# Two transformer layers as one block: borders crossed by token tile, gate and up products with the weights stationary

## What is computed

```
def hybrid_layer(x, c, ada_w, ada_b, ...):
    mod = jax.nn.silu(c) @ ada_w + ada_b
    sh_m, sc_m, g_m, sh_f, sc_f, g_f = [m[:, None, :] for m in jnp.split(mod, N_MOD, axis=-1)]
    h = rms_norm(x, norm_mix_g) * (1 + sc_m) + sh_m
    proj = h @ w_in
    ...
    merged = (jax.nn.sigmoid(ga) * (o_na @ w_br_na)
              + jax.nn.sigmoid(gb) * (o_mla @ w_br_mla)
              + jax.nn.sigmoid(gc) * (o_gqa @ w_br_gqa))
    x = x + g_m * (merged @ w_out)
    h = rms_norm(x, norm_ffn_g) * (1 + sc_f) + sh_f
    gate, up = jnp.split(h @ ffn_w_gate_up, 2, axis=-1)
    x = x + g_f * ((jax.nn.silu(gate) * up) @ ffn_w_down)
    return x
```

## Time and profile before

| | |
|---|---|
| median of 3 runs | 1840.91 us |
| the profiled execution's own time | 1846.1 us |
| its span, first to last instruction | 1844.3 us |
| TensorE matmuls busy | 88% of the span |
| VectorE busy | 66% |
| ScalarE busy | 44% |
| mean granted TensorE clock | 0.925 of full |

### The profile page before, as it was taken

One profiled execution on the slowest core, in us unless ns is written; L12 is line 12 of the kernel. 1 busy time (PEld: TensorE's weight loads), 2 busy tenths in 40 slices (PEclk: granted clock), 3 DMA queues, 4 the chain that ended last, 5 costly groups with the idle time before them and its releaser, 6 DMA issues. The chain is left out here.

```text
span 1844.3 us, 25528 instructions
## 1 busy us (share of the span) xinstructions
PE 1625.5 (88%) x10701; PEld 1469.1 (80%) x10701; DVE 1225.5 (66%) x1338; ACT 813.2 (44%) x921; POOL 35.7 (2%) x52
## 2 busy tenths in 40 slices
PE   2899998999899999899969997897698958999995
PEld 2789887999788988799969997885687856888884
DVE  4777577787656547566554876534565757898895
ACT  1345434333244543433323562225433316777673
POOL 0100000000010000000000000000000000000000
PEclk8899998999989999899989998987887968999998
DMA  8975337888744324466446462111222446999992
GB/s 307 298 231 159 139 118 258 296 305 301 248 140 146 114 89 154 169 206 227 139 122 200 143 183 92 46 46 46 85 76 69 137 139 217 367 358 359 355 358 108
DMA packets 226057, 348.07 MB, mean 189 GB/s; under 512 B 14612, under 2 KB 156672, under 8 KB 225808
## 3 DMA queue, kind: packets, MB, share of 16 engines
q1 hardware_dynamic: 225936, 346.36, 56.0%
HBM read 345.29 MB, written 1.97 MB: 188 GB/s over the span
## 5 line engine op out<-in xcount | busy, mean ns | idle before, releaser
L458 PE MATMUL bank<-layer_split,hT_pair 128*128 128x256 f32 (+1 forms) x4224 | 511.1, 281 | 9.9 <-DVE hT_pair L315 5.5
L458 PEld LDWEIGHTS bank<-layer_split,hT_pair 128*128 128x128 f32 x4224 | 496.9, 190 | 16.6 <-issue 9.3
L184 DVE TENSOR_TENSOR layer_split<-layer_raw,layer_split 128x2048 fp32r<-128x2048 f32 x122 | 280.2, 2296 | 99.0 <-ACT layer_split L172 97.4
L172 ACT ACTIVATE layer_split<-layer_raw 128x2048 fp32r<-128x2048 f32 x122 | 233.7, 1915 | 199.3 <-PE bank L458 114.4
L184 DVE TENSOR_TENSOR expert_split<-expert_raw,expert_split 128x2048 fp32r<-128x2048 f32 x96 | 219.4, 2289 | 40.8 <-ACT expert_split L172 40.7
L172 ACT ACTIVATE expert_split<-expert_raw 128x2048 fp32r<-128x2048 f32 x96 | 184.2, 1920 | 76.5 <-PE bank L1823 39.1
L458 PE MATMUL bank<-split_w,hT_pair 128*128 128x256 f32 (+1 forms) x1248 | 183.9, 311 | 13.9 <-PEq L2018 5.0
L458 PEld LDWEIGHTS bank<-split_w,hT_pair 128*128 128x128 f32 x1248 | 173.2, 207 | 25.1 <-issue 15.6
L184 DVE TENSOR_TENSOR split_w<-raw_w,split_w 128x2048 fp32r<-128x2048 f32 x52 | 119.2, 2292 | 66.8 <-ACT split_w L172 66.2
L672 PE MATMUL bank<-layer_split,ffnh_aT 128*128 128x512 f32 x528 | 127.0, 396 | 2.8 <-DVE ffnh_aT L744 2.8
L172 ACT ACTIVATE split_w<-raw_w 128x2048 fp32r<-128x2048 f32 x52 | 99.4, 1911 | 59.7 <-PE bank L458 52.4
(11 more groups left out here) (442 smaller groups left out, 1783.7 us busy)
## 6 DMA issues: line engine op xcount, KB each, us to landing
layer_raw<-in_ada_w SPq DMA_DIRECT2D x48, 1024.0 KB, 5.9
layer_raw<-in_ffn_w_gate_up SPq DMA_DIRECT2D x44, 1024.0 KB, 5.1
raw_w<-in_w_in SPq DMA_DIRECT2D x40, 1024.0 KB, 5.1
layer_raw<-in_w_in SPq DMA_DIRECT2D x38, 1024.0 KB, 6.1
expert_raw<-in_w_gate SPq DMA_DIRECT2D x32, 1024.0 KB, 7.2
expert_raw<-in_w_up SPq DMA_DIRECT2D x32, 1024.0 KB, 7.2
expert_raw<-in_w_down SPq DMA_DIRECT2D x32, 1024.0 KB, 6.9
layer_raw<-in_ffn_w_down SPq DMA_DIRECT2D x22, 1024.0 KB, 5.1
```

What stands on the lines that cost most here:

```text
L172: self.nc.scalar.activation(self.pair[:, j % self.pairs, 0, 0:self.size[n]], self.raw[:, n % self.depth, 0:self.size[n]], ACT.Copy).then_i ...
L184: self.nc.vector.tensor_tensor(self.pair[:, j % self.pairs, 1, 0:self.size[n]], self.raw[:, n % self.depth, 0:self.size[n]], self.pair[:, ...
L458: ins = nc.tensor.matmul(out, lhs, rhs, start=c == 0 and tp + wp == 0, stop=c == job.k - 1 and tp == 1)
```

## The change

Five things are done at once. (1) Both layers stand in one `nc.Block`; each engine runs `proj`, `att`, `ffn` of layer 0 and then of layer 1 with no barrier between. (2) At the borders the work goes by token tile: `SkewNorm` squares halves of a tile, normalises tile 0 and later tile 1, and ScalarE writes the scaled value, from which VectorE copies the high half and subtracts the low one. The output product is ordered by tile pairs; the transposes of the heads' results stand among the heads (three of four) and those of the merged sum among the branch products (`Merge`). (3) The gate and up products have the weights stationary and 256 tokens moving; their result has features on partitions, so the four transposes per block are gone. ScalarE applies SiLU in one activation (before, a sigmoid, and VectorE multiplied), VectorE multiplies once instead of twice, and the high half is copied from SBUF. (4) In the first block of each feed-forward part the tokens move by tile: `hidden_of_tile`, 192 products of 128 columns in place of 96 of 256. (5) The projections use their weight units in another order (2, 3, 0, 1, 4 ...).

```diff
-                for c0 in range(0, 1952, 256):
-                    w["proj"].append(add_cols("w_in", l, c0, min(c0 + 256, 1952)))
-                    ada_next(p)
+                w["proj"] = [None] * 8
+                for i in (2, 3, 0, 1, 4, 5, 6, 7):
+                    w["proj"][i] = add_cols("w_in", l, 256 * i, min(256 * i + 256, 1952))
+                    ada_next(p)
...
-                        attention(l, ring, w, cols_l[l], mods[l], Gm[l], gate_rows, ada, rows_loaded, make_strips, sg3, o_tok, x_in)
-                        merge(ring, w, sg3, o_tok, gate_rows[:, 0, :])
-                        norm = Norm("ffn", s2, ring, w["gu"][0][0], Gf[l], mods[l][:, 24:32])
-                        gated_hidden("ffnh", ring, (lambda n, up, w=w: w["gu"][n][up], lambda n, w=w: w["dn"][n]), n_hidden,
-                                     lambda n, t: None, norm=norm, ada=ada, sync_first=rows_ahead, gate=gate_rows[:, 1, :], tail=1 + l)
...
+                    def rows_ahead(sp, l=l, merge=merge):
+                        sp.wait_ge(merge.out_left.sem, 8)
+                        if l + 1 < DEPTH:
+                            load_gate_row(sp, l + 1, 2, rows_loaded)
+                            make_strips(sp, l + 1)
+                        load_gate_row(sp, l, 5, rows_loaded)
+                    ffn = FeedForward(ring, w, n_hidden, buf, ffn_norm[l], mix_norm[l + 1] if l + 1 < DEPTH else None, ada,
+                                      rows_ahead, gate_rows[:, 1, :])
+                    parts += [proj, att, ffn]
+                LAYER[0] = ""
...
+                    @block.tensor
+                    def _(pe):
+                        for part in parts:
+                            part.tensor(pe)
...
+            def flat(self, act, t, half):
+                act.wait_ge(self.turned, 2 * t + half + 1)
+                act.wait_ge(*self.scale_ready)
+                for k in range(4 * half, 4 * half + 4):
+                    ins = nc.scalar.activation(self.xn[t][:, k * P:(k + 1) * P], ps[4 + 2 * t + half][:, (k % 4) * P:(k % 4 + 1) * P],
+                                               ACT.Identity, bias=self.bias[:, k:k + 1], scale=self.scale[:, k:k + 1])
+                ins.then_inc(self.flat_out, 1)
+            def vector(self, dve, t, half):
+                dve.wait_ge(self.flat_out, 2 * t + half + 1)
+                src = self.xn[t][:, 512 * half:512 * half + 512].rearrange("p (k s) -> p k s", k=4)
+                hi, lo = (hP[:, i, 4 * half:4 * half + 4, t * P:(t + 1) * P] for i in range(2))
+                done(dve, nc.vector.tensor_copy(hi, src), self.split)
+                nc.vector.tensor_tensor(lo, src, hi.bitcast(FP), ALU.subtract).then_inc(self.lo_out, 1)
+            def ready(self, t):
+                def wait(pe, c):
+                    if c % 4 == 0:
+                        pe.wait_ge(self.lo_out, 2 * t + c // 4 + 1)
+                return wait
...
+                self.branch(pe, 10)
+                self.turn_half(pe, 2)
+                self.branch(pe, 11)
+                self.output(pe, 0)
+                self.turn_half(pe, 3)
+                for j in range(1, 7):
+                    self.output(pe, j)
+                self.output(pe, 7, lambda: self.norm.turn(pe, 0))
+                self.norm.turn(pe, 1)
...
+                self.hi_half(act, 3)
+                norm.square(act, 0, 0)
+                ring.hi(act, w["out"][3])
+                norm.square(act, 1, 0)
+                ring.hi(act, w["gu"][0][0])
+                norm.square(act, 0, 1)
+                norm.flat(act, 0, 0)
+                norm.flat(act, 0, 1)
+                norm.square(act, 1, 1)
+                ring.hi(act, w["gu"][0][1])
+                norm.flat(act, 1, 0)
+                norm.flat(act, 1, 1)
...
+                self.output_out(dve, 1)
+                ring.lo(dve, w["out"][3])
+                self.output_out(dve, 2)
+                self.output_out(dve, 3)
+                ring.lo(dve, w["gu"][0][0])
+                self.output_out(dve, 4)
+                self.output_out(dve, 5)
+                norm.norm(dve, 0)
+                self.output_out(dve, 6)
+                norm.vector(dve, 0, 0)
+                norm.vector(dve, 0, 1)
+                self.output_out(dve, 7)
+                ring.lo(dve, w["gu"][0][1])
+                norm.norm(dve, 1)
+                norm.vector(dve, 1, 0)
+                norm.vector(dve, 1, 1)
...
+                def hidden_of_tile(up, t):
+                    ring.arrived(pe, gu(0, up))
+                    weights = [ring.view(gu(0, up), wp, KD, UNIT_W) for wp in range(2)]
+                    for f in range(2):
+                        for c in range(KD):
+                            if up + f == 0:
+                                norm.ready(t)(pe, c)
+                            for tp, wp in ((0, 0), (0, 1), (1, 0)):
+                                ins = nc.tensor.matmul(ps[up][:, f * S + t * P:f * S + (t + 1) * P],
+                                                       weights[wp][:, c, f * P:(f + 1) * P], hP[:, tp, c, t * P:(t + 1) * P],
+                                                       start=c + tp + wp == 0, stop=c == KD - 1 and tp == 1)
+                    if t == 1:
+                        ins.then_inc(ring.used, 1)
...
+                for n in range(blocks):
+                    if n == 0:
+                        for up, t in ((0, 0), (1, 0), (0, 1), (1, 1)):
+                            hidden_of_tile(up, t)
+                    else:
+                        hidden(n, 0)
+                        hidden(n, 1)
+                    if n and ada.due(gu(n, 0)):
+                        ada.reduce(pe, 3, 1)
+                        self.reduced_in[n] = 1
+                    if n >= 1:
+                        down(n - 1)
+                down(blocks - 1)
+                while ada.due(ring.ahead(dn(blocks - 1), 1)):
+                    ada.reduce(pe, 3, 1)
+                self.ada_end = ada.done_pe
+                if self.norm_next is not None:
+                    self.norm_next.turn(pe, 0)
+                    self.norm_next.turn(pe, 1)
...
+                for n in range(self.blocks):
+                    ring.hi(act, ring.ahead(gu(n, 0), 2))
+                    act.wait_ge(ring.used, ring.uses(gu(n, 0)))
+                    if n >= 1:
+                        act.wait_ge(self.acted, n)
+                    nc.scalar.activation(self.sig.rearrange(flat), ps[0][:, :], ACT.Silu).then_inc(self.gated, 1)
+                    ring.hi(act, ring.ahead(gu(n, 0), 3))
+                    act.wait_ge(self.acted, n + 1)
+                    if n >= 1:
+                        act.wait_ge(ring.used, ring.uses(dn(n - 1)))
+                    ring.hi(act, ring.ahead(gu(n, 1), 3))
+                    nc.scalar.activation(self.aT[:, 0, :, :].rearrange(flat), self.a.rearrange(flat), ACT.Copy) \
+                        .then_inc(self.hi_out, 1)
+                    if n >= 1:
+                        ring.hi(act, ring.ahead(dn(n - 1), 3))
...
+                for n in range(self.blocks):
+                    ring.lo(dve, ring.ahead(gu(n, 0), 2))
+                    if n and self.reduced_in[n - 1]:
+                        ada.leave(dve, 3)
+                    ring.lo(dve, ring.ahead(gu(n, 0), 3))
+                    dve.wait_ge(self.gated, n + 1)
+                    dve.wait_ge(ring.used, ring.uses(gu(n, 1)))
+                    if n >= 1:
+                        dve.wait_ge(self.lo_out, n)
+                    nc.vector.tensor_tensor(self.a.rearrange(flat), ps[1][:, :], self.sig.rearrange(flat), ALU.mult) \
+                        .then_inc(self.acted, 1)
+                    ring.lo(dve, ring.ahead(gu(n, 1), 3))
+                    dve.wait_ge(self.hi_out, n + 1)
+                    nc.vector.tensor_tensor(self.aT[:, 1, :, :].rearrange(flat), self.a.rearrange(flat),
+                                            self.aT[:, 0, :, :].rearrange(flat).bitcast(FP), ALU.subtract).then_inc(self.lo_out, 1)
+                    if n >= 1:
+                        ring.lo(dve, ring.ahead(dn(n - 1), 3))
+                dve.wait_ge(self.tile_sum, 1)
+                self.add(dve, 0, 0)
+                self.add(dve, 0, 1)
+                dve.wait_ge(ring.used, ring.uses(dn(self.blocks - 1)))
+                self.add(dve, 1, 0)
+                if norm is not None:
+                    norm.norm(dve, 0)
+                self.add(dve, 1, 1)
+                while ada.done_dve < self.ada_end:
+                    ada.leave(dve, 3)
+                if norm is not None:
+                    norm.vector(dve, 0, 0)
+                    norm.vector(dve, 0, 1)
+                    norm.norm(dve, 1)
+                    norm.vector(dve, 1, 0)
+                    norm.vector(dve, 1, 1)
```

1202 lines of the change are left out of this document (774 added, 428 removed).

## The result

The changed kernel takes 1897.2 us (median of 4 executions, 1889.03 to 1900.38) against 1841.99 for the kernel before in the same series: ratio 1.0285, 95% interval 1.0259 to 1.0311. It is slower by 3%; I had forecast 1837.0 with a range to 1850. The profiled execution took 1895.74 us, its span is 1893.9, its mean granted clock 0.912.

The account below looks back on a forecast made before the run. Inside the stages TensorE was taken as the bound (transfers at the start). Terms 1.7 + 2.6 + 1.6 - 6.4 + 3.0 - 0.6 - 5.75 = -3.85 us gave 1842.2 on the profiled scale, 1837.0 on the median's; range 1826 to 1850.

Parts of the forecast that it names:

- The part between heads and output product: Layer 0, last head's transposes to the end of the output products: 55.0 us instead of 60.4, a gain of 5.4.
- The entry: Start of the feed-forward part: 8.5 us stop, then low clock and narrow products, 33.9 us against 26.75, loss 7.1.
- I take 5.5 in all, nearer to the unbroken case: Low-clock time after the feed-forward entry's stop: 2.0 us of transposes plus 3.5 us of products, bounded by 4.0 and 14.6.
- Rival B: Feed-forward entries: low clock outlasts 5.5 us, each further microsecond costing half; at 14.6 us, 9 us more, 1846; chance 0.20.
- Rival C: First feed-forward blocks: stationary loads hide, narrow products run at 0.09 us, 8.6 us less, 1828.4; chance 0.08.
- E: Feed-forward entries: ScalarE and VectorE run ahead, half of the two 8.5 us stops goes, 1828.5; chance 0.12.
- D: Steady blocks: 1.3 us slack fails, units come 2.5 us late, ten blocks lose 1.2 us each, 1849; chance 0.15.
- the term of -6.4: Steady feed-forward blocks: four transposes less save 0.36 us a block, nine blocks in each of two layers, -6.4 us.
- Weights or tokens stationary makes no difference: Steady feed-forward blocks: 256-column products were to take the same time with either operand stationary.
- Around the last down product: Stop ahead of it: 5.0 us in layer 0, +3.0; 1.4 us in layer 1, -0.6; layer 0's product takes 8.0 us.
- The border to layer 1: Last down product to the first 96 projection products: 9.3 us until tile 1 is turned, 32.1 against 37.85, -5.75 us.

Follow-up runs that it names:

- wide: Changed kernel with the first feed-forward block as 96 products of 256 columns, started once both tiles are split: 1843.3 us, ratio 1.0018 to the kernel before.
- narrow-first: Kernel before with only each layer's first feed-forward block made of 192 products of 128 columns instead of 96 of 256: 1892.5 us, ratio 1.0285.
- gate-wide: Changed kernel with the first block's gate product as 48 products of 256 columns, its up product still 96 of 128 behind it: 1849.4 us, one execution.
- the sixth block: Kernel before with only each layer's sixth feed-forward block made of 192 products of 128 columns instead of 96 of 256: 1862.0 us, ratio 1.0126.
- the tokens-stationary run: Changed kernel with tokens stationary and weights moving in gate and up products from the second block on, output not the reference's: 1882.5 us.
- the fastest version: Changed kernel with the feed-forward entry stop taken away, first up product 256 columns wide, ScalarE's high half ahead of its wait: 1833.5 us, ratio 0.9963.
- the run without the stop: Changed kernel, first block still narrow, with ScalarE and VectorE reordered and tile 1 turned after tile 0's first 48 products: 1844.9 us, ratio 1.0014.

## Why the prediction was wrong

**The part between heads and output product: wrong.** Forecast 55.0 us, measured 60.2 (222.59 to 282.80), so the gain of 5.4 never was. The waits were right (4.7 us idle for 4.3 and hops). The work was mis-sized, TensorE was busy 55.5 and not about 50 us. Twelve products of 512 columns behind the 0.95 us stop took 4.44 us, at the low clock (at my 0.229 each it would be 2.7), the rest 0.237 each; the output products come every 0.120 us and not 0.1145; the transposes of tile 0 ran at the low clock. For the 512-column products I had doubled a price of 256-column ones, though the kernel before has their own row, 0.238 each:

```profile
234.48 22.83 PE L458 MATMUL bank<-layer_split,merge_pair 128*128 128x512 f32 x96 [0.22 <-DVE merge_pair L315]
```

**The entry: the failed step.** The stop was right (8.01 and 7.82 us for 8.5), and so was the price of a narrow product at full clock. Wrong was "I take 5.5 in all, nearer to the unbroken case", with its reason that the low clock ends with unbroken work. Between the transposes' start and the rise of the clock lie 45.7 us of unbroken work. The wide, narrow-first and gate-wide runs show what was missing: the time at the low clock depends on what runs, and these products of 128 columns seldom end it. Both rows from which I bounded it, 4.0 and 14.6 us (14.9 by its own row, 0.57 being the mean of that microsecond), end in 256-column products; I carried the bound over to narrow ones without saying so. The cost is 42.6 us where I had 25.4, in each layer. The Trainium skill, TensorE: Matmul & The Clock Gate, What's actually happening, has the warm-up as a matter of time and not of how many products, with one count for 128 columns and one for 512. By that rule the clock would have been full early in the first block, and my 5.5 us were drawn up the same way. The trace disagrees (41.0 us at 0.50 with 128 columns, 3 to 5 us with 256), and the trace decides.

What it is about these products stays open, for 128 columns alone don't do it: in the kernel before, rows of 16 transposes of 128 columns see the clock rise within them, at 263.5 and 744.7. Widths between 128 and 256 weren't run. But the trace of the kernel before holds a warning that I passed over, in its second part: 16 transposes and 32 products of 16 columns, 10.3 us without a gap, and the clock stays at 0.50.

```profile
1500.50 3.68 PE L1682 MATMUL bank<-cst,x 128*128 128x128 f32 x16 [12.91 <-DVE x L1613]
1503.97 6.85 PE L1692 MATMUL bank<-router_w,hT 128*128 128x16 f32 x32
```

```profile
1500.50:1510.80 10.30, 10.30 (x48) 10.21 (x48) 5.10 (x5) 4.55 (x6) 0.00 (x0) 0.50 0.85 330
```

**Rival B had the mechanism.** "Slower, by the clock alone", with every further microsecond costing half of one: 40 us more than my 5.5 in each layer make 2 x 20 = 40 on top of 1842.2, 1882. Its size stopped at 14.6 us for the same reason. Rival C (narrow products at 0.09 us) is refuted by the 21.63 us of the sixth block; E by the stops; D did not happen, no steady block shows a wait for a low half.

**Steady blocks: the term of -6.4 was nothing.** The period is 16.78 us (831.86 to 848.64), before it was 16.81 (848.01 to 864.82). "Weights or tokens stationary makes no difference" holds, the tokens-stationary run shows it; but the pace of products of one shape is not a constant. It is 113 ns in the next layer's 96 projection products (553.64, 11.05 us), 118 in the steady blocks (11.47). What sets it stays open. Tried and ruled out are the order within a group, the stationary operand, and transposes ahead; with other kernels the same rows switch between the two values (96 projections 11.47 us in one version, 11.05 in the others; the block behind the entry of the tokens-stationary run 11.10, and with four transposes on the fastest version 11.13), so neither the shape nor the place in the program fixes it. The other engines' work beside it was not varied, and each kernel was profiled once, so these rows don't tell whether such a switch belongs to a kernel or to an execution.

**Around the last down product: right in layer 0** (4.98 us forecast 5.0, 7.65 for 8.0) and in layer 1 (1.50 for 1.4). Of the +4.2 us before it 3.0 are this stop and 1.4 the low clock in the second block.

**The border to layer 1: -0.9 for -5.75.** I left out that the reduction of the adaptive vector (16 products, 1.84 us) stays on this path: it waits 5.13 us for VectorE and runs 3.55 us at the low clock, ahead of the transposes of tile 0. The tile 1 transposes start 14.9 us after the last down product ends, not 9.3.

**What remains of the change.** With the wide first block it is level with the kernel before; with only the gate product narrow and the orders on ScalarE and VectorE mended it is 0.4% faster. The one block that moves by tile costs 54 of the 55 us.

## What to carry to other kernels

Where a change puts narrower products behind a stop, don't take the time at the low clock from rows of wide products: look through the whole trace, other stages too, for narrow work that begins at clock 0.50, and if there is none, keep a forecast in which the whole row is slow. If work must go tile by tile there, put the wide products first (or soon after) and the narrow ones behind them. And before a chain of small gains is summed, check that the pace of the long rows is the same in every stage of the trace.

## What the runs showed of the hardware

- 128-column products (fp32 operands in split halves, one weight load each): 0.2135 us at clock 0.50 (192 in 41.20 us), 0.1125 at 1.00 (192 in 21.63); 256-column ones 0.113 to 0.120 at 1.00. Against 0.118 the narrower product saves 5% at full clock, for half the work.
- Of 14 rows of 192 narrow products behind stops of 4.4 to 8.9 us, 12 stayed at 0.50 for their 41 us, one fell to it after 2.4 us and stayed, one came up. Rows of 256-column products that began at 0.50 in the first block or right behind it reached 1.00 after 2.1 to 6.3 us in every trace (the wide first block: 298.19 to 301.1).
- The clock can also fall within narrow work: at 282 us in the run without the stop, after gaps of 0.47 and 1.13 us, while the same code in layer 1 (one gap of 1.13 us, one of 0.64) kept it. Of five traces with these two gaps in layer 0, three lost it in the first narrow row.
- 256-column products at full clock come every 113, 118 or 120 ns. Most rows keep one pace; the 192 projection products of the changed kernel's layer 1 (564.52, 22.45 us) go at 118 and, towards their end, at 113. What sets the pace is open.
